# Prompt attention with the rotary score as a 128-row matmul on zero-padded keys

## What is computed

```
s = (jnp.einsum('bqhd,bkhd->bhqk', qn, k_nope)
     + jnp.einsum('bqhr,bkr->bhqk', qr, k_rope)).astype(jnp.float32) * ATTN_SCALE
mask = kpos[None, :] <= qpos[:, None]
s = jnp.where(mask[None, None], s, -jnp.inf)
p = jax.nn.softmax(s, axis=-1).astype(v.dtype)
return jnp.einsum('bhqk,bkhd->bqhd', p, v)
```

## Time and profile before

| | |
|---|---|
| median of 3 runs | 2146.16 us (2145.61 to 2154.82) |
| span of the profiled execution, first to last instruction | 2144.2 us |
| PE, weight loads, DVE, ACT busy | 95%, 92%, 48%, 37% |
| mean granted TensorE clock | 0.973 |
| prompt attention, from its first score to the last `o_lo` | 653.21 to 704.80 us |

### The profile page before, as it was taken

How to read it: one execution, slowest core, us unless ns; L and a number is a source line. 1 busy time by engine, 2 the same in 40 slices (tenths; PEclk the granted TensorE clock), 3 DMA queues, 4 the chain that set the end, 5 groups by cost and what they waited for, 6 DMA issues and landing times.

```text
span 2144.2 us, 34292 instructions
## 1 busy us (share of the span) xinstructions
PE 2028.8 (95%) x13392; PEld 1964.5 (92%) x13392; DVE 1029.1 (48%) x1220; ACT 798.7 (37%) x952; POOL 162.6 (8%) x212
## 2 busy tenths in 40 slices
PE   5899999999999799999995999999999999999996
PEld 3899999999996688899895999999999999999996
DVE  6465324333335355145446455455554555555547
ACT  4345553332344444133233333324333333343332
POOL 3010000000000000000002201101001011010010
PEclk9999999999999899899997999999999999999998
DMA  4334344443442367534443244443443443434342
GB/s 171 114 141 171 127 156 149 145 156 141 153 173 103 111 215 245 177 137 149 175 151 110 101 154 146 149 150 144 145 148 144 149 155 138 156 137 156 138 153 98
DMA packets 58017, 318.05 MB, mean 148 GB/s; under 512 B 6450, under 2 KB 6642, under 8 KB 24818
## 3 DMA queue, kind: packets, MB, share of 16 engines
q1 hardware_dynamic: 57314, 313.15, 40.9%
q10 hardware_dynamic: 656, 4.27, 0.5%
HBM read 313.08 MB, written 4.32 MB: 148 GB/s over the span
## 4 chain that ended last, share of the span: by engine, by line
PE 91%; DVE 4%; issue 2%; ACT 1%; DMA 1%; POOL 1%; SPq 0%; ACTq 0%; DVEq 0%
PE ps L1054 90%; POOL h_lo L347 1%; DVE sq L762 1%; ACT w_hi L416 1%; DVE norm_tmp L706 1%; DVE w_lo L706 0%; PE ps L1288 0%; DVE x L1047 0%; DMA xT<-in_x 0%; PE ps L1201 0%; DVE x L706 0%; DVE rstd L749 0%; DMA w_raw<-in_cache_t 0%; DMA c_raw<-in_cache 0%; DVE pool_ta L706 0%
## 5 line engine op out<-in xcount | busy, mean ns | idle before, releaser
L706 DVE TENSOR_TENSOR w_lo<-w_raw,w_hi 128x2048 fp32r<-128x2048 f32 x266 | 609.9, 2293 | 751.8 <-ACT w_hi L416 751.6
L1054 PE MATMUL ps<-h_hi,w_hi 128*128 128x320 f32 x2512 | 750.9, 312 | 46.2 <-ACT h_hi L416 21.1
L416 ACT ACTIVATE w_hi<-w_raw 128x2048 fp32r<-128x2048 f32 x266 | 508.4, 1912 | 709.1 <-PE ps L1054 702.4
L1054 PE MATMUL ps<-h_lo,w_hi 128*128 128x320 f32 x2512 | 746.9, 311 | 0.0
L1054 PEld LDWEIGHTS ps<-h_hi,w_hi 128*128 128x128 f32 x2512 | 477.3, 190 | 56.5 <-issue 46.1
L1054 PEld LDWEIGHTS ps<-h_lo,w_hi 128*128 128x128 f32 x2512 | 477.5, 190 | 0.2 <-issue 0.2
L1054 PE MATMUL ps<-h_hi,w_lo 128*128 128x320 f32 x2512 | 394.9, 308 | 0.0
L1054 PEld LDWEIGHTS ps<-h_hi,w_lo 128*128 128x128 f32 x2512 | 376.2, 188 | 0.0
L1054 PE MATMUL ps<-hid_hi,w_hi 128*128 128x320 f32 x704 | 217.0, 308 | 0.0
L1054 PE MATMUL ps<-hid_lo,w_hi 128*128 128x320 f32 x704 | 216.9, 308 | 0.0
L1054 PE MATMUL ps<-hid_hi,w_lo 128*128 128x320 f32 x704 | 216.9, 308 | 0.0
(11 more groups left out here) (188 smaller groups left out, 1849.5 us busy)
## 6 DMA issues: line engine op xcount, KB each, us to landing
w_raw<-in_slabs SPq DMA_DIRECT2D x254, 1024.0 KB, 4.8
w_raw<-in_cache_t SPq DMA_DIRECT2D x64, 288.0 KB, 3.6
c_raw<-in_cache SPq DMA_DIRECT2D x64, 256.0 KB, 3.7
w_whole<-in_slabs SPq DMA_DIRECT2D x4, 1024.0 KB, 7.0
xT<-in_x SPq DMA_DIRECT2D x4, 640.0 KB, 6.1
x_again<-in_x ACTq DMA_DIRECT2D x1, 2560.0 KB, 10.9
out_y<-x SPq DMA_DIRECT2D x4, 640.0 KB, 3.2
cst<-in_consts SPq DMA_DIRECT2D x1, 651.5 KB
```

The costliest lines, as they stand in the source:

```text
L416: return nc.scalar.activation(out, in_, ACT.Copy)
L706: return nc.vector.tensor_tensor(out, a, b, op)
L1054: return nc.tensor.matmul(out, a, b, start=start, stop=stop, **kw)
```

## The change

The rotary key gets a second copy, `kr_half`, with two planes of 128 x 256. Plane 0 has the key in partitions 0 to 63 and zeros in the others; plane 1 has zeros in 0 to 63 and the key in 64 to 127. The rotary matmul then takes all 128 partitions of the tile of two heads' queries as its stationary operand, and plane i % 2 as its moving operand; the other head's queries meet zeros. The four instructions that fill the planes stand on DVE behind the split of the second slab. A semaphore `kr_halves` covers them, and PE waits for it once, at the head of the stage. The sample part's own rotary matmuls still use 64 rows.

```diff
@@ -178,6 +178,7 @@
         kr = sb("kr", [P, T])
+        kr_half = sb("kr_half", [P, 2, NP])
@@ -222,6 +223,7 @@
         kr_copied, kr_step, kr_ready = sem("kr_copied"), sem("kr_step"), sem("kr_ready")
+        kr_halves = sem("kr_halves")
@@ -866,6 +868,11 @@
             tt(kr[:, :], kr[:, :], qsw[:, 0, :], ALU.add).then_inc(kr_ready, 1)
             split(g + 3)
+            dve.wait_ge(kr_ready, 1)
+            for odd in range(2):
+                here, other = 64 * odd, 64 * (1 - odd)
+                nc.vector.memset(kr_half[other:other + 64, odd, :], 0.0)
+                nc.vector.tensor_copy(kr_half[here:here + 64, odd, :], kr[here:here + 64, 0:NP]).then_inc(kr_halves, 1)
             for t in range(PT_):
@@ -1181,16 +1188,15 @@
             pe.wait_ge(kr_ready, 1)
+            pe.wait_ge(kr_halves, 2)
             for i in range(H + 3):
                 if i < H:
                     if i >= 2:
                         pe.wait_ge(sc_masked, i - 1)
-                    r0 = 64 * (i % 2)
                     for q in range(2):
                         out = ps[:, 2 + i % 2, q * P:q * P + (q + 1) * P]
                         mm(out, qn[:, i, q * P:q * P + P], kT[:, i, 0:(q + 1) * P], True, False)
-                        last = mm(out, qr[r0:r0 + 64, i // 2, q * P:q * P + P], kr[r0:r0 + 64, 0:(q + 1) * P],
-                                  False, True)
+                        last = mm(out, qr[:, i // 2, q * P:q * P + P], kr_half[:, i % 2, 0:(q + 1) * P], False, True)
                     last.then_inc(sc_done, 1)
```

## The result

| | before | changed |
|---|---|---|
| median, us | 2149.7 (2144.72 to 2154.82, 8 runs) | 2137.19 (2134.62 to 2143.58, 8 runs) |
| ratio of the times | | 0.9942 [0.9924, 0.9961] |
| profiled execution: time, span | -, 2144.2 | 2137.37, 2135.6 |
| mean granted TensorE clock | 0.973 | 0.974 |
| attention, first score to last `o_lo` | 51.59 | 42.94 |

The profiled spans differ by 8.6 us, and the attention stage alone by 8.65. The medians differ by 12.5 us, 0.58%. The difference comes from the times of before, which lie in two groups: four from 2144.72 to 2146.16 and four from 2153.24 to 2154.82. Their lower four have a median of 2145.6, 8.4 above the changed kernel's.

A forecast was written before the change was run, and what follows sets the result against it. PE was taken to bound the attention stage, losing time at row-count changes. Start 2.3 plus heads 5 to 15 6.4 gave 8.7 us, so 2146.2 - 8.7 = 2137.5 us, range 2134.5 to 2143.0.

The forecast's parts named there:

- What bounds the stage, and why: Prompt attention: PE bounds at 3.03 us a head; four changes between 128 and 64 rows each expose a weight load and refill.
- PE's own work of a head, 2.28: Prompt attention on PE: scores 1.30, transposes 0.33, product with values 0.65 us, together 2.28 in place of 3.03.
- The wait that comes next: Round trip through DVE and ACT: PE waits 0.23 us for `pt`; two heads take 4.90, saving 6.4 us over heads 5 to 15.
- The start and the end: Attention stage: scores of heads 0 to 4 gain 2.3 us; the tail from head 15's mask keeps its length.
- The added work on DVE: Fill ahead of the first `op_lo`: up to 1.5 us, costed at nothing behind 1.6 us of cover before `gate_b`'s second slab.
- The rule against the change: Skill page: weight loads overlap running matmuls only when the row group differs, so padded matmuls would never have a load hidden.
- Rival (d): Prompt scores: no load overlaps on shared rows, scores 2.08 against 1.98 us, 1.6 us slower, 2147.8; chance 0.02.
- The size on the clock's side: Whole kernel: median 2.0 us above the profiled span, so 2146.2 - 8.7 = 2137.5 us, 0.4% faster; within 0.5% had chance 0.82.
- Rival (e): `ukt`, behind attention: the shifted tail lets the clock fall to 1.2 GHz, costing 11.3 us more, 2148.8; chance 0.06.
- (a): Attention stage: the round trip is shorter and PE alone bounds, gaining 10.5 us, 2135.7; chance 0.13.
- (b): Prompt scores: the load goes ahead only in part, or operand changes cost part; half the gain, 2141.8; chance 0.14.
- (c): Prompt scores: rotary loads stay late for a cause other than their rows, no gain, 2146.2; chance 0.08.

## Why the prediction was right, point by point

- **What bounds the stage, and why.** Right. The cost sits at the changes of row count: two changes fewer saved 0.39 us (0.19 each), four saved 0.73 (3.03 to the 2.30 that the run with ACT's copy first shows), 0.18 each. The late load is the sign of a change; what else is in the 0.18 us beside the 0.11 that a load otherwise runs ahead is not shown. The Trainium skill, page "TensorEngine Tiling (Array Packing)", section Key Properties, says that changing the tiling mode drains the engine. The rows here fit that, at 0.18 to 0.19 us for a change, though no row shows a drain as such.
- **PE's own work of a head, 2.28.** Measured 2.30. Scores 1.30 were 1.31 to 1.32; transposes 0.33 and product 0.65 as forecast.
- **The wait that comes next.** Right in place and size: 0.23 us at every other head, on ACT's `pt`, and the product behind it 0.75 for 0.76. A round is 4.92 for 4.90.
- **The start and the end.** Scores of heads 0 to 4 end 663.55 - 654.14 = 9.41 us after the first, for 9.46. From the last head's mask to the end of the stage it is 697.08 - 690.67 = 6.41, and 704.80 - 698.38 = 6.42 before. Before, the scores of heads 0 to 4 took 664.98 - 653.21 = 11.77 us, so the start gains 2.36 us for 2.3, and the steady part 6.3 for 6.4. Sum: 8.65 us for 8.7.
- **The added work on DVE.** Right that it is hidden. The release moved by 1.4, within the bound of 1.5, and stood at 220.25 rather than "near 219", since in this execution `gate_b` began 0.8 us later. The prices were too high: the copy took 0.29 where 0.42 was taken from the earlier trace rows, a mean over 32 copies that a few long ones raise (the longest took 1.35 us, the middle one 0.29), and the memset 0.27 for 0.33. The gaps of 0.2 us, which had no term, made up for most of that.
- **The rule against the change.** Rival (d) did not come: `kr_half` loads run 0.11 us ahead of their matmuls, on the same 128 rows as the matmul before them. The Trainium skill, page "TensorE: Matmul & The Clock Gate", section The mechanism, has the rule in its list, that a load overlaps running matmuls only when the row group differs. Its opening paragraph is wider and also lets a load go ahead that targets the background weight buffer. The rows here contradict the rule as the list has it, and the measurement decides; they do not show which buffer a load targets.
- **The size on the clock's side.** Here the prediction was incomplete. The time of 2137.5 was met (2137.19), but that it was met to 0.3 us is luck: the changed kernel's own times run from 2133.35 to 2143.58. And "the median stands 2.0 above that span, so 2146.2 - 8.7" took the median of three as that of before, which by chance came from the lower group. Over eight runs it is 2149.7, since four of the eight are of the upper group, which lies some 9 us higher, as the one profile of it does by its stage. So the measured ratio says 0.58% faster, just over the line of 0.5%, where "within 0.5%" had the chance of 0.82; its interval has both sides of the line. Rival (e) named 2154.82 as perhaps of its kind, a cold `ukt`. If that execution was like the one profiled, the mechanism was right (a stage at 1.2 GHz) and its place was not; in the changed kernel rival (e) did not come.
- **Rivals (a), (b), (c)** fell by the period: 2.46, not 2.28, and not 2.75 or more. What (a) describes, PE alone as the bound, came once ACT's order was changed: the stage was then 11.1 us shorter than before, for 10.5.

## What to carry to other kernels

Where matmuls of 64 rows stand between matmuls of 128, compare the starts of the weight loads with those of their matmuls: a load that starts with its matmul marks a change that costs some 0.19 us here. Padding the short ones with zeros to 128 rows removes it at no cost in columns, and where zeros can't be had, putting the short ones side by side removes half, as the run with two changes shows for the time (its output was wrong, so each sum would need a place where the other does not disturb it). When one engine has been made faster, work out the round trip through the others before the sum: here 0.16 us of the 0.73 a head that PE could save went into the wait for ACT, and moving one copy gave it back. A median of three can come from one of two groups of times, so look at the clock of each execution before you count from it.

## What the runs showed of the hardware

- The attention stage of the kernel before, all matmuls and a wait of 1.18 us ahead of it, was granted 1.00 throughout in three of four profiled executions and 0.50 over its first heads, for some 20 us of unbroken work, in the fourth. This cost 9.1 us (60.68 and 51.59). By the times alone, 18 of 38 executions may have been like the fourth.
- `uv2` fell to half clock after its first matmuls in 13 of 14 profiled executions and stayed at 1.00 in one of the kernel before, worth 11.5 us (25.8 and 14.3): the difference between two executions of one kernel (2134.68 and 2154.06 here) can be larger than the change itself.
- A change between 64 and 128 rows costs less in the sample part, 0.57 / 4 = 0.14 us, than in the prompt's scores, 0.18 to 0.19. What makes the difference was not tried.
